# Pages turned three steps ahead, and projection products spread as 3.5 and 4.5 pieces a step

## What is computed

```python
h = rmsnorm(x, norm_g)
proj = jnp.einsum('bsd,de->bse', h, w_in)
q, k, v, g_a, u, v_s, g_b, m_a, m_b = jnp.split(proj, SPLIT_POINTS, axis=-1)
# mixer A, prompt: block-sparse causal attention over own and selected blocks of 256
# mixer A, samples: the 3 best of 8 cached blocks by q . mean(k), then softmax over them and the new rows
k_full = cache_k[layer, page_table[:, :n_full * ppb]]
gate = jnp.einsum('bthd,bnhd->bhtn', q, k_mean)
_, sel = lax.top_k(gate, n_sel)
p = jax.nn.softmax(jnp.concatenate([s_sel, s_loc], axis=-1), axis=-1)
# mixer B: u * (tril(w_s) @ layernorm(gelu(v_s)) + b_s), in chunks of 128
mixed = sigmoid(m_a) * (attn * silu(g_a)) @ w_pa + sigmoid(m_b) * (sgu * silu(g_b)) @ w_pb
y = rmsnorm(x + mixed @ w_o, final_norm_g)
```

## Time and profile before

| | before |
|---|---|
| time, median of 3 runs | 547.55 us (544.87 to 548.51) |
| profiled execution: time, span | 548.5 us, 546.7 us |
| TensorE busy in the span | 519.2 us (95%) |
| VectorE, ScalarE, GpSimd busy | 307.8, 179.7, 121.2 us (56%, 33%, 22%) |
| mean TensorE clock granted | 0.986 of full speed |
| moved by DMA | 112.00 MB, mean 205 GB/s |
| page turns L1332, 128 of them | 87.9 us busy, mean 699 ns |

### The profile page before, as it was taken

One profiled execution on the slowest core, in us unless ns is written; L12 is line 12 of the kernel. 1 busy time (PEld: TensorE's weight loads), 2 busy tenths in 40 slices (PEclk: granted clock), 3 DMA queues, 4 the chain that ended last, 5 costly groups with the idle time before them and its releaser, 6 DMA issues.

```text
span 546.7 us, 13830 instructions
## 1 busy us (share of the span) xinstructions
PE 519.2 (95%) x5624; PEld 474.6 (87%) x5624; DVE 307.8 (56%) x686; ACT 179.7 (33%) x389; POOL 121.2 (22%) x108
## 2 busy tenths in 40 slices
PE   8999999999999999999979689989979999999993
PEld 6999999989899999998979689879978999998672
DVE  6624333476765655766833767985433454784524
ACT  5522222233433432454442241212151141343313
POOL 1201111331411411321231235422360300000002
PEclk9999999999999999999999999989997999999998
DMA  8645533377648778677498998877798792360004
GB/s 253 183 155 169 182 119 119 103 229 250 195 153 272 224 252 292 200 237 247 145 334 259 302 306 285 252 245 220 255 308 292 228 330 79 126 230 1 2 10 153
DMA packets 73561, 112.00 MB, mean 205 GB/s; under 512 B 5501, under 2 KB 35338, under 8 KB 73498
## 3 DMA queue, kind: packets, MB, share of 16 engines
q1 hardware_dynamic: 72122, 107.51, 60.4%
q0 software_dynamic: 1232, 3.36, 2.1%
q10 hardware_dynamic: 144, 0.26, 0.1%
HBM read 106.57 MB, written 4.53 MB: 203 GB/s over the span
## 4 chain that ended last, share of the span: by engine, by line
PE 78%; DVE 8%; DMA 7%; SPq 3%; issue 2%; ACT 0%; POOL 0%; POOLq 0%; DVEq 0%; ACTq 0%
PE BK L583 36%; PE BK L603 9%; PE BK L922 8%; DMA KRAW<-in_cache_k 7%; PE BK L737 4%; PE BK L751 4%; PE BK L672 2%; DVE KT L1332 2%; PE BK L799 2%; PE BK L816 2%; PE BK L617 2%; PE BK L806 2%; SPq L511 1%; PE BK L852 1%; PE BK L779 1%
## 5 line engine op out<-in xcount | busy, mean ns | idle before, releaser
L583 PE MATMUL BK<-XH,WH 128*128 128x272 f32 x672 | 202.9, 302 | 0.0
L583 PE MATMUL BK<-XL,WH 128*128 128x272 f32 x672 | 194.5, 289 | 0.0
L583 PE MATMUL BK<-XH,WL 128*128 128x272 f32 x672 | 194.5, 289 | 0.0
L583 PEld LDWEIGHTS BK<-XH,WH 128*128 128x128 f32 x672 | 127.8, 190 | 10.8 <-issue 10.0
L583 PEld LDWEIGHTS BK<-XL,WH 128*128 128x128 f32 x672 | 127.7, 190 | 0.0
L583 PEld LDWEIGHTS BK<-XH,WL 128*128 128x128 f32 x672 | 127.4, 190 | 0.0
L1695 POOL TENSOR_TENSOR WL<-WRAW,WH 128x1024 fp32r<-128x1024 f32 x32 | 76.7, 2396 | 207.9 <-ACT WH L971 207.9
L1332 DVE STREAM_TRANSPOSE KT<-KRAW 128x512 f32<-128x512 f32 x128 | 87.9, 699 | 55.1 <-DMA KRAW<-in_cache_k 54.6
L971 ACT ACTIVATE WH<-WRAW 128x1024 fp32r<-128x1024 f32 x52 | 55.0, 1057 | 15.6 <-PE BK L603 15.6
L737 PE MATMUL BK<-KT,QW 128*32 128x128 f32 x1024 | 35.0, 278 | 15.5 <-DVE KT L1332 15.5
L737 PEld LDWEIGHTS BK<-KT,QW 128*32 128x32 f32 x1024 | 26.2, 110 | 20.8 <-DVE KT L1332 17.0
(11 more groups left out here) (207 smaller groups left out, 810.5 us busy)
## 6 DMA issues: line engine op xcount, KB each, us to landing
KRAW<-in_cache_k SPq DMA_DIRECT2D x128, 256.0 KB, 4.6
WRAW<-in_w_in SPq DMA_DIRECT2D x21, 1024.0 KB, 7.8
VRAW<-in_cache_v SPq DMA_DIRECT2D x56, 256.0 KB, 3.5
VQT<-in_cache_v SPq DMA_DIRECT2D x28, 256.0 KB, 4.1
VEX<-in_cache_v SPq DMA_DIRECT2D x24, 256.0 KB, 3.8
VGU<-in_cache_v SPq DMA_DIRECT2D x20, 256.0 KB, 3.7
WO<-in_w_o SPq DMA_DIRECT2D x4, 1024.0 KB, 6.3
XR<-in_x_prompt SPq DMA_DIRECT2D x4, 512.0 KB, 4.9
```

Source lines behind the costliest of these rows:

```text
L583: last = mm(BK[h][:, 0:HALF], w[:, n % 2, k, :], x[:, k, cols], start=(i == 0 and w is WH and x is XA), stop=(i == KC - 1 and w is WL))
```

## The change

Pages are turned three steps before their own step (`AHEAD = 3`): steps 0, 1 and 2 turn two pages each, step t then page t + 3, and step 125 and later none. Page loads move with the turns, since each follows the turn that frees its buffer. TensorE's filling is 4 and 3 pieces in even and odd steps up to 63, and 4 and 5 from 64 to 127. Everything that hangs on a tile's end (evictions, splits, weight loads, GELU, gate product) is placed by `evict_step`, the first step after the tile's last piece. Chunk mixing stands four steps later, and three value loads that wait for it two steps later. A new semaphore `rh_ok` keeps the scores of a sample's third page group behind VectorE's maximum over the first two, which the earlier turns no longer order.

```diff
+AHEAD = 3
+def pieces_at(t):
+    return 4 - t % 2 if t < 64 else 4 + t % 2 if t < PAGES else 4
+def evict_step(n, h):
+    if n < N_QKV:
+        return 0
+    left, t = 16 * (n - N_QKV) + 8 * h + 8, 0
+    while left > 0:
+        left -= pieces_at(t)
+        t += 1
+    return t
+def turned_at(t):
+    return [i for i in ((2 * t, 2 * t + 1) if t < AHEAD else (t + AHEAD,)) if i < PAGES]
@@ load_step
-    first = {1: 8, 11: 64, 25: 113, 26: 115, 27: 117}
+    first = {1: 8, 11: 64, 25: 115, 26: 117, 27: 119}
@@ sync
-                if t + KR < PAGES:
-                    load_k(t + KR)
-                if t % 8 == 2:
-                    load_w(8 + t // 8)
+                for i in turned_at(t):
+                    if i + KR < PAGES:
+                        load_k(i + KR)
+                for m in range(8, 26):
+                    if t == (evict_step(2 * m - 5, 1) + 2 if m < 25 else 138):
+                        load_w(m)
@@ tensor, page_scores
+                if x == 2:
+                    pe.wait_ge(rh_ok, b + 1)
@@ tensor, loop
-                run(fill, 2)
+                run(fill, 2 if t % 2 == 0 or t >= PAGES else 1 if t < 64 else 3)
...
-                if t in (100, 102, 104, 106, 108):
-                    spatial((t - 100) // 2)
+                if t in (104, 106, 108, 110, 112):
+                    spatial((t - 104) // 2)
@@ scalar, loop
-                n = N_QKV + t // 4
-                if t % 4 == 0 and 4 <= t <= 128:
-                    evict(n - 1, 1)
-                    split_hi(n + 1)
-                if t % 4 == 2 and t < 128:
-                    evict(n, 0)
+                for n, h in halves_at(t):
+                    evict(n, h)
+                for n in splits_at(t):
+                    split_hi(n)
@@ vector, page_sums
-                if x == 1:
+                if x == 0:
+                    peak.then_inc(rh_ok, 1)
+                else:
                     link(peak)
@@ vector, loop
-                if t < PAGES:
-                    page_turn(t)
-                if t % 4 == 0 and 4 <= t <= 128:
-                    if T_GA <= n - 1 < T_GMA or T_GB <= n - 1 < T_GMB:
-                        silu(n - 1, 1)
+                for i in turned_at(t):
+                    page_turn(i)
+                for n, h in halves_at(t):
+                    if T_GA <= n < T_GMA or T_GB <= n < T_GMB:
+                        silu(n, h)
@@ gpsimd, loop
-                if t % 4 == 0:
-                    split_lo(N_QKV + t // 4 + 1)
+                for n in splits_at(t):
+                    split_lo(n)
```

More of the change, by code:

```diff
@@ L164, in evictions_before, with halves_at, splits_at, tile_at @@
     return min(n, T_PB) + max(n - T_WO, 0)
+def pieces_at(t):
[8 more added lines that the diff above has]
+    return t
+def halves_at(t):
+    return [(n, h) for n in range(N_QKV, T_PB) for h in range(2) if evict_step(n, h) == t]
+def splits_at(t):
+    return [n + 2 for n in range(N_QKV, T_PB) if evict_step(n, 1) == t]
+def tile_at(t, first, count, after):
+    for x in range(count):
+        if evict_step(first + x, 1) + after == t:
+            return x
+    return None
 def values_step(q):
@@ L410, in build @@
         kt_ok, sc_pe, qr_pe, qr_ok, qw_ok, bw_ok = sem("kt_ok"), sem("sc_pe"), sem("qr_pe"), sem("qr_ok"), sem("qw_ok"), sem("bw_ok")
-        r_ok, gm_pe, gm_ev, eb_ok, ex_ok = sem("r_ok"), sem("gm_pe"), sem("gm_ev"), sem("eb_ok"), sem("ex_ok")
+        rh_ok, r_ok, gm_pe, gm_ev, eb_ok, ex_ok = sem("rh_ok"), sem("r_ok"), sem("gm_pe"), sem("gm_ev"), sem("eb_ok"), sem("ex_ok")
         pt_pe, pt_ok, pl_ok, lm_pe, rl_ok = sem("pt_pe"), sem("pt_ok"), sem("pl_ok"), sem("lm_pe"), sem("rl_ok")
@@ L1142, in _ @@
                     probs_out(sample_at(t, probs_step))
-                if t % 4 == 1 and 53 <= t < 85:
-                    gelu_square((t - 53) // 4)
-                if t % 4 == 2 and 54 <= t < 86:
-                    gelu_tanh((t - 54) // 4)
+                if tile_at(t, T_GV, 8, 1) is not None:
+                    gelu_square(tile_at(t, T_GV, 8, 1))
+                if tile_at(t, T_GV, 8, 2) is not None:
+                    gelu_tanh(tile_at(t, T_GV, 8, 2))
                 if t == 117:
@@ L1549, in _ @@
                     prompt_gate(block_at(t - 5))
-                if t % 4 == 2 and t < 128 and (T_GA <= n < T_GMA or T_GB <= n < T_GMB):
-                    silu(n, 0)
                 if block_at(t - 2) is not None:
@@ L1568, in _ @@
                     prompt_max(block_at(t))
-                if t % 4 == 2 and 54 <= t < 86:
-                    gelu_inner((t - 54) // 4)
-                if t % 4 == 3 and 55 <= t < 87:
-                    gelu_outer((t - 55) // 4)
+                if tile_at(t, T_GV, 8, 2) is not None:
+                    gelu_inner(tile_at(t, T_GV, 8, 2))
+                if tile_at(t, T_GV, 8, 3) is not None:
+                    gelu_outer(tile_at(t, T_GV, 8, 3))
                 if t == 88:
@@ L1580, in _ @@
                     norm_scale((t - 94) // 2)
-                if t in (101, 103, 105, 107, 109):
-                    spatial((t - 101) // 2)
+                if t in (105, 107, 109, 111, 113):
+                    spatial((t - 105) // 2)
                 if 133 <= t < 133 + PAIRS:
@@ L1718, in _ @@
             for t in range(4, 129):
-                if t % 4 == 0:
-                    split_lo(N_QKV + t // 4 + 1)
+                for n in splits_at(t):
+                    split_lo(n)
                 if t % 16 == 1 and t > 16 and t < 128:
                     query_rows(t // 16)
-                if t % 4 == 1 and 85 <= t < 101:
-                    gate_product((t - 85) // 4)
+                if tile_at(t, T_GB, 4, 1) is not None:
+                    gate_product(tile_at(t, T_GB, 4, 1))
                 if t in (91, 93, 95, 97, 99):
```

1 line of the change is left out of this document (removed).

## The result

The changed kernel takes 540.28 us (median of 11 runs, 539.0 to 542.48) where the kernel before took 548.35 us on the same chip (median of 11, 543.5 to 551.87): a ratio of 0.9866, 95% interval 0.9841 to 0.9891. That is faster by 1.3%, some 8 us, and a little over half of the 14.5 us that the prediction summed up; the median lies 2.3 us above its range of 529 to 538 us. The span fell from 546.7 to 537.2 us.

What follows compares the result with a forecast made beforehand. TensorE bounds the kernel, with 22.0 us of the second stage not work. Terms -15.5 - 5.1 + 3.4 + 1.7 + 1.0 = -14.5 us: span 546.7 to 532.2, time 533.0 us, range 529 to 538.

Steps and rivals of the forecast that it cites:

- The place and kind of the hole: Second stage, steps 64 to 127: TensorE's page scores wait 15.5 us for pages turned by VectorE; all should go.
- A wait of about 2 us for a silu near 108 to 111 us: Loop start: TensorE waits for the first silu eviction behind seven page turns; a sign that the forecast is right.
- the first stage: Steps 0 to 63: about 150 to 153 us if the forecast is right; 157 us or more if wrong.
- the gate sums' 1.4: Two TensorE waits for VectorE's row sums in the second stage, 1.4 us, left as they are in the sum.
- with those waits gone I expect the clock to stay at 2.4 GHz: 5.1 us back: Two falls to 1.2 GHz after waits in the second stage lose 1.7 and 3.4 us; both should go.
- new waits in the second stage, 1.0 us, bounds 0 and 5: Silu evictions move later behind selection, normalisation and two turns, with one step of cover at worst: 1.0 us lost.
- the late page of 305 us: Page turned at 304.33; its load, issued behind a 1 MB weight load, took almost 9 us against a median of 4.6.
- the waits move: Rival: TensorE meets VectorE's lateness at evictions and gate sums; half of 15.5 us stays, about 545 us; chance 0.13.
- the rival beside GpSimd: Rival: scalings on VectorE delayed beside GpSimd's splits, two delays adding 4.1 us, 537 us; chance 0.08.
- The prompt chain: First stage, twelve prompt blocks passing between PE, VectorE and ScalarE with little slack: 1.7 us lost, bounds 0 and 12.
- its 1.4 at the start: Page 8 stands ahead of the first prompt maximum; the chain to normalisation ends about 1.4 us later than wanted.
- 285 is possible: Second stage's DMA demand of about 285 GB/s held possible, since 295 GB/s were moved in 411 to 420 us.

Runs made afterwards that it cites:

- experiment 11: Experiment 5's kernel with the WSB product that TensorE waits for put ahead of GELU's passes in VectorE's step 89: 533.27 us, ratio 0.9727 to the kernel before.
- experiment 2: Changed kernel with each page turned in its own step (AHEAD = 0), uneven filling kept: 547.97 us, ratio 0.9992 to the kernel before.
- experiment 4: Changed kernel with the four setup loads of step 72 issued in steps 78 and 83: 539.35 us, ratio 0.9816 to the kernel before.
- experiment 6: Changed kernel with the two GELU passes ahead of the page turns in VectorE's step: 539.56 us, ratio 0.9851 to the kernel before.
- experiment 1: Changed kernel with the uneven filling undone, four pieces in every step, pages still turned three steps ahead: 543.67 us, ratio 0.9898 to the kernel before.
- experiment 5: Changed kernel with the three-page lead built in steps 8, 16 and 24 and setup loads moved to steps 78 and 83: 534.2 us, ratio 0.9752 to the kernel before.
- experiment 12: Experiment 11's kernel with the loop's weight loads also cut into quarters, one a step: 533.59 us, ratio 0.9716 to the kernel before.
- experiment 10: Changed kernel with each 1 MB weight load of the loop cut into four, issued one a step: 539.26 us, ratio 0.9829 to the kernel before.
- experiment 7: The changed kernel measured again, unaltered, beside others of its group: 539.78 us, ratio 0.9865 to the kernel before.

## Why the prediction was right, and where it was not

**Right.** The place and kind of the hole: all 15.5 us of page-score waits went, with VectorE's waits for pages unchanged (54.6 to 53.7 us, expected 30 to 55). A wait of about 2 us for a silu near 108 to 111 us came with 2.85, and the gain of over 1%, to which the prediction gave a chance of 0.82, came. The work doesn't change: the steps of the second stage became longer and those of the first shorter by what 3.5 and 4.5 pieces give. The page scores of steps 64 and 128 in TensorE's timeline of the changed kernel:

```profile
255.92 1.08 PE L782 MATMUL BK<-KT,QW 128*32 128x128 f32 x32
421.59 1.08 PE L782 MATMUL BK<-KT,QW 128*32 128x128 f32 x32
```

The same two in the kernel of experiment 11:

```profile
252.90 1.08 PE L784 MATMUL BK<-KT,QW 128*32 128x128 f32 x32
415.70 1.08 PE L784 MATMUL BK<-KT,QW 128*32 128x128 f32 x32
```

From about 101.4 us the first stage takes 154.5 us in the changed kernel and 151.5 in experiment 11 (expected 150 to 153), the second 165.7 and 162.8 (161 to 163). Experiment 11 has the span (531.3) and the time (533.27) that the prediction gave the change itself (532.2, 533.0). The sum's work was right to within 1 to 2 us, and its stalls were wrong. That the two spans agree to 0.9 us is in part luck: experiment 11 still waits 5.1 us in the loop where the sum had 7.5 (3.4, 1.7, 1.0 and the gate sums' 1.4), and holds 1.7 us outside of the waits that the count has not.

**Mis-sized: "with those waits gone I expect the clock to stay at 2.4 GHz: 5.1 us back".** 1.7 us came back. The prediction put a wait of 2 us at the start into its own sum, 2.85 came, and the clock fell behind it as it had fallen behind 2.66 us before. The price of such a wait was the wait and 1.7 us; only the first was counted, and the 5.1 us had no bounds. This is 3.4 us of the miss, at two waits.

**Mis-sized: "new waits in the second stage, 1.0 us, bounds 0 and 5".** 4.7 us: 2.71 + 0.49 + 1.50. The step looked at the silu evictions, which stand behind turns on VectorE. It overlooked the link by which ScalarE's evictions stand behind VectorE too: tanh waits for GELU's first pass. It also put the late page of 305 us down to a 1 MB weight load alone, where the four setup loads of step 72 stand right ahead of it in the queue (experiment 2, the trace of before) and VectorE waited 7.55 us behind them. And it took up to four steps of cover as the end of the danger, which is so for the pages alone: everything else in VectorE's queue still stands behind a turn that may wait. Experiment 2 shows that the early turns aren't needed for it (1.67 us at the same eviction); they and the steps moved for the filling together make 2.71. A late page met at an eviction is the rival "the waits move", which was priced at half of the 15.5 us and came with 3.2, at the GELU eviction. Experiments 4 and 6 show both ends of this chain. The other 1.50 us is the rival beside GpSimd, at a GELU pass instead of the scalings that it named: one delay of 2.1 us, 1.5 of it on the path. Experiment 2 shows that the moved steps bring it, not the turns.

**Over-sized: the first stage and the gate sums.** The prompt chain waits 0.9 us (0.7 at the turns, 0.2 at the scores), 0.7 more than the 0.2 before, instead of 1.7 more, and its 1.4 at the start did not show beside the 2.85 (3.4 were set for both). The gate sums' 1.4 us, left as they were in the sum, went.

Put together, waits fell by 17.1 - 8.4 = 8.7 us (the 16.9 and 0.2 at a prompt turn before) and the loss to the clock by 1.7: 10.4, where the span fell by 9.5. Some 0.2 us of the difference lies ahead of the loop, the remaining 0.7 us I have not traced. Against the predicted 14.5 that is 3.4 (clock) and 3.7 (second stage) missing, and 0.6 (start) + 1.0 (prompt chain) + 1.4 (gate sums) on the other side. The prediction also stood on a median of 547.55 us from three runs; eleven runs gave 548.35. Its bounds were added up wrongly: the upper ones (6, 12 and 5 us) give about 550 us, not 541, and the stated range of 529 to 538 is narrower than either.

**Not settled.** Why the clock fell behind some waits and not behind others (below). Whether four page buffers are what keeps VectorE waiting for pages. And the kernel of experiment 11 still waits 1.6 us at prompt turns, 1.5 at gate sums and 1.3 at a silu eviction; nothing was tried against these.

## What to carry to other kernels

When work is pulled ahead in an in-order queue to hide its lateness, price everything that stands behind it: the pulled work gains slack, its neighbours don't, and where they are moved too, or many pulled items are put ahead of one of them at once, they lose some; their dependants may sit on a third engine. A late item is then felt at whichever consumer comes first. Build such a lead gradually and place large one-off loads away from it: these two edits of the program's order brought 5.6 us more in one group (539.78 to 534.2 us), two thirds as much again as the change. A TensorE wait of some 1.7 us or more in a kernel that keeps TensorE busy has to be priced with the half clock that may come behind it.

## What the runs showed of the hardware

- A stretch of half clock inside the loop came only behind or within a wait of TensorE: behind 2.66 and 3.49 us before, 2.85 and 2.71 after, 6.61 in experiment 1, and also behind 1.82 us (experiment 5) and 1.67 us (experiment 2, at 292.72, clock 0.82 in 292 to 297). It did not come behind 3.00 and 3.67 us at 285 and 305 us before, nor behind 2.53 us in experiment 12 (clock 1.00 in the 10 us around each). The wait's length alone doesn't decide.
- Ahead of the loop it came without a wait: in experiments 4, 5, 6 and 10 the clock is 0.83 in 36 to 46 us, with TensorE busy for 10.00 of the 10 us; in the kernel before it is 1.00 there. The same instructions run there in all of them, with narrow products of 32 rows just ahead of the fall.
- A VectorE pass with both operands in the on-chip buffer (128x544 f32, 0.73 us alone) took 2.85 and 1.87 us beside a GpSimd split and ended 0.58 and 0.57 us behind the split's end; a 32x256 product with one operand in an accumulation bank took 0.39 us in the middle of a split (experiment 11).
- The same waits come back within 0.3 us in another execution (experiment 7), while the half clock behind them lasts once or twice as long. Much of the spread between runs of one kernel can be this: experiment 5 ran from 532.0 to 536.49 us, with spans of 530.2 us at a mean clock of 0.997 and 534.7 at 0.992.
- DMA moved 376 GB/s over 10 us (294 to 304 in the changed kernel), well over the 295 GB/s on which the prediction had rested that 285 is possible.
